# A two-block fp32 network on one core: projections merged into the differential attention, a reordered opening, and stage beginnings that run two or three tiles side by side

## The chip, the core and the metric

The kernel runs on one core of one Trainium2 chip. The metric is the device time of one execution in microseconds (us). A core has TensorE (PE in the rows: matrix products; PEld is its weight load), VectorE (DVE), ScalarE (ACT), GpSimd (POOL) and SyncE (SP, which starts DMAs). Each engine works through its own instructions in their order and waits on semaphores. TensorE's clock has two levels, 1.2 and 2.4 GHz; "granted clock" is its mean share of full speed in a stretch.

## The reference

Everything is fp32, batch 1, 256 tokens, width 1024. Cut to what matters:

```python
# block one
xn = rmsnorm(h, norm_mix_g)
q_a, k_a, v_a, q_b, f_b, i_b, og_b, g_a, g_b = split_cols(xn @ w_in)      # nine projections of 1024
y_a = moba_attention(q_a, k_a, v_a, positions) @ w_br_attn                 # "attention A": 16 heads of 64, causal, rope
y_b = hgrn2(q_b, f_b, i_b, og_b, lb, hgrn_norm_g) @ w_br_hgrn              # gated linear recurrence, 8 heads of 128
h = h + (sigmoid(g_a) * y_a + sigmoid(g_b) * y_b) @ w_out
h = h + memory_cross_attention(rmsnorm(h, g_x), rmsnorm(mem, g_mem), wq_x, wkv_x, wo_x)   # 4 heads of 256
hn = rmsnorm(h, norm_ffn_g)
h = h + (silu(hn @ w_gate) * (hn @ w_up)) @ w_ffn_out
x2 = rmsnorm(h, final_norm_g)
# block two, layer 0: differential attention over 256 tokens and 256 context tokens
q, k, v, z = split(adaln_norm(t) @ w_in0)          # for the tokens and for the context
o = softmax(q1 k1) v - lam * softmax(q2 k2) v      # 8 heads, two softmaxes of 64 each
o = rms_norm(o, subln_g) * (1 - lam_init)
y = (o * silu(z)) @ w_out0
# block two, layer 1: 8 query heads on 2 key heads (GQA), then the same gating and w_out1
```

## The kernel before

Activations lie feature-major: [128 partitions, k, tokens], with k = 0..7 the eight slices of 128 features. A projection of 1024 features is eight **tiles** (t = 0..7), each a weight piece of 128 x 1024. An fp32 product is made of three fp32r products: w_hi by X_H, w_hi by X_L, w_lo by X_H (L1040 to L1042), where H is the operand cast to fp32r and L the rest. A tile is so 8 x 3 = 24 products, 256 columns wide, or 512 where tokens and context go together (names W in block two). A weight piece lands in a ring of seven buffers (w_raw), ScalarE casts w_hi (L1263), VectorE subtracts w_lo (L1450), into a ring of four; tiles are summed in three PSUM banks named lin.

The program is one list, `steps`. Each engine walks the whole list in its order and carries out what is its own in each step. So the place of a step in the list is its place in every engine's queue. Steps are: "lin" (a tile, with its evacuation: a copy, a scaling "R", silu, gating, and so on), "gain" and "shift" (making the operand H and L of one k), "sq"/"sqmm" (squares and their sums), "rt" (GpSimd's power for the norm), "bc", "rope", "score_mm", "score_exp", "pscale", "transp", "values", "values_out", "headn", "zgate". Weights are split ahead of use: at the lin step of a tile, the tiles up to two further are split, and this split stands ahead of the tile's own evacuation; with `HL` four pieces can be live.

`bc` spreads a norm's 1/rms over all partitions: VectorE multiplies the identity by the 128 values (L1568, tile diag), TensorE multiplies ones by that (L1116), VectorE copies the result to rstd (L1570).

The opening makes eight gain steps (XH, XL), 8 x 2 sums of squares, then q_a; after its first tile a "setup" step makes the rope's angles, sines and the attention's lambda. Ropes of q_a's tiles stand in q_a, those of k_a's in k_a. An attention is a pipeline over (head, part): while one softmax is scaled and transposed, the scores of the next are made, and `fill()` puts other work between "values" and "transp". In attention A `fill_w` puts three tiles of q_b ... g_b into each head until the 44 tile steps are used up. HGRN then has 14 rounds (`htake`), each followed by one tile of k_x or v_x; the operand of mem (eight gains, MH, ML) is made before. `pending` holds evacuations put off by one round.

In block two all of q_2, k_2 and v_2 stand ahead of the differential attention, whose `fill_da` holds only norm steps; its scores use a ring of four banks. All z_2 tiles come after, each evacuated through silu and the gating with the head's output (zgate: L1527, L1491, L1492, 512 wide, making ZH and ZL), then w_out0 twice (the two halves st of 256 tokens), q_3, k_3, v_3, the GQA attention with z_3 in it, eight gates, and w_out1. TensorE waits for all eight gates of w_out0 at once, and in w_out1's first tile for one gate per k. Where a tile's operand has just been made, the first tile waits for each k in turn.

## Time and profile before

| | us |
|---|---|
| median of 3 runs | 1445.77 (1445.62 to 1447.35) |
| profiled execution, its own time | 1446.14 |
| its span in the trace | 1444.4 |
| TensorE busy | 1262.5 (87%) |
| VectorE busy | 819.7 (57%) |
| ScalarE busy | 598.8 (41%) |
| differential attention with q_2, k_2, v_2 before it and z_2 behind | 850.8 to 1179.5 |

Times in the trace count from the span's start. "Stretches" give, for a window, each engine's busy time and TensorE's granted clock; timeline rows give one instruction, or a run of like ones, with the idle time of its engine before it and the instruction that ended it.

### The profile page before, as it was taken

To read this page: it belongs to the slowest core of one execution; us is meant where nothing else is said; L and a number is where in the kernel's file an instruction comes from. 1 tells how busy PE (TensorE), PEld (TensorE's weight loads), DVE (VectorE), ACT (ScalarE), POOL (GpSimd) and SP (SyncE) were. 2 spreads that over 40 slices of the span, in tenths; PEclk is the share of its full clock that TensorE was granted. 3 is DMA by queue.
4 is the path that set the end of the run, shared out by engine and by line. 5 is a ranking of instruction groups with operands and counts; after the bars stand their busy time and mean duration, and the time that the engine had idled before them with its cause. 6 is when DMAs were issued, how large, how long until landed. Compare 5 with 4: busy or idle time off the path is not lost.

```text
span 1444.4 us, 22626 instructions
## 1 busy us (share of the span) xinstructions
PE 1262.5 (87%) x8530; PEld 1116.0 (77%) x8530; DVE 819.7 (57%) x1604; ACT 598.8 (41%) x1077; POOL 53.4 (4%) x51
## 2 busy tenths in 40 slices
PE   4999998988875998999998979998776899888886
PEld 4998997978874997988897968895333679887766
DVE  4755554659655755565665444425777445575563
ACT  4864445451311343433333335634444235454452
POOL 0000000002021000000000000000000000001000
PEclk9999999998987999999999979998887899879988
DMA  6454443442311452488865722230000124312110
GB/s 234 145 170 148 134 148 128 139 139 72 104 59 44 149 177 74 132 292 292 293 229 214 258 87 89 101 103 30 1 0 1 44 90 158 103 59 74 62 42 30
DMA packets 48395, 175.01 MB, mean 121 GB/s; under 512 B 5376, under 2 KB 6016, under 8 KB 47776
## 3 DMA queue, kind: packets, MB, share of 16 engines
q1 hardware_dynamic: 47664, 169.77, 34.7%
q0 software_dynamic: 624, 3.80, 0.7%
q8 instruction: 69, 1.13, 0.3%
q14 instruction: 38, 0.31, 0.1%
HBM read 172.50 MB, written 1.05 MB: 120 GB/s over the span
## 4 chain that ended last, share of the span: by engine, by line
PE 38%; issue 11%; DVE 7%; ACT 2%; POOL 0%; ACTq 0%; POOLq 0%; DVEq 0%
PE lin L1040 10%; PE lin L1042 9%; PE lin L1041 9%; PE sum_bank L1104 1%; DVE stat L1692 1%; PE lin L1055 1%; PE lin L1057 1%; PE lin L1056 1%; PE o_bank L1153 1%; PE score L1073 1%; PE sum_bank L1116 1%; ACT probs L1385 1%; DVE probs L1716 1%; DVE diag L1568 0%; DVE probs L1635 0%
## 5 line engine op out<-in xcount | busy, mean ns | idle before, releaser
L1450 DVE TENSOR_TENSOR w_lo<-w_raw,w_hi 128x1024 fp32r<-128x1024 f32 (+1 forms) x272 | 328.5, 1213 | 225.4 <-ACT w_hi L1263 185.6
L1263 ACT CAST w_hi<-w_raw 128x1024 fp32r<-128x1024 f32 (+1 forms) x272 | 275.5, 1036 | 120.3 <-PE lin L1042 87.2
L1040 PE MATMUL lin<-XH,w_hi 128*128 128x256 f32 x448 | 131.5, 293 | 3.2 <-DVE w_lo L1450 3.1
L1041 PE MATMUL lin<-XL,w_hi 128*128 128x256 f32 x448 | 128.8, 287 | 0.0
L1042 PE MATMUL lin<-XH,w_lo 128*128 128x256 f32 x448 | 128.7, 287 | 0.0
L1040 PE MATMUL lin<-NH,w_hi 128*128 128x256 f32 x416 | 121.5, 292 | 0.0
L1041 PE MATMUL lin<-NL,w_hi 128*128 128x256 f32 x416 | 119.0, 286 | 0.0
L1042 PE MATMUL lin<-NH,w_lo 128*128 128x256 f32 x416 | 118.9, 286 | 0.0
L1104 PEld LDWEIGHTS sum_bank<-ones,sqr 128*128 128x128 f32 x368 | 55.5, 225 | 49.5 <-ACT sqr L1297 48.9
L1040 PEld LDWEIGHTS lin<-XH,w_hi 128*128 128x128 f32 x448 | 88.2, 197 | 7.1 <-issue 6.7
L1104 PE MATMUL sum_bank<-ones,sqr 128*128 128x2 f32 x368 | 55.6, 266 | 40.6 <-ACT sqr L1297 40.2
L1040 PEld LDWEIGHTS lin<-NH,w_hi 128*128 128x128 f32 x416 | 80.9, 194 | 12.7 <-issue 12.6
L1041 PEld LDWEIGHTS lin<-XL,w_hi 128*128 128x128 f32 x448 | 88.1, 197 | 0.0
L1042 PEld LDWEIGHTS lin<-XH,w_lo 128*128 128x128 f32 x448 | 88.0, 196 | 0.0
L1042 PEld LDWEIGHTS lin<-NH,w_lo 128*128 128x128 f32 x416 | 81.1, 195 | 0.0
L1041 PEld LDWEIGHTS lin<-NL,w_hi 128*128 128x128 f32 x416 | 81.0, 195 | 0.1
L1040 PE MATMUL lin<-WH,w_hi 128*128 128x512 f32 x192 | 78.7, 410 | 2.7 <-DVE WL L1608 2.7
L1041 PE MATMUL lin<-WL,w_hi 128*128 128x512 f32 x192 | 76.5, 398 | 0.0
L1042 PE MATMUL lin<-WH,w_lo 128*128 128x512 f32 x192 | 76.4, 398 | 0.0
L1219 POOL TENSOR_TENSOR ms<-ms,mhalf 128x4 f32<-128x4 f32 (+1 forms) x26 | 26.2, 1008 | 1300.8 <-DVE ms L1558 1300.8
L1385 ACT ACTIVATE probs<-score,stat 128x512 f32<-128x512 f32 (+1 forms) x56 | 34.6, 621 | 69.2 <-DVE stat L1697 42.7
L1143 PE MATMUL pt_bank<-ident,probs 128*128 128x128 f32 x224 | 39.1, 299 | 24.0 <-DVE probs L1721 22.0
(350 smaller groups left out, 3231.4 us busy)
## 6 DMA issues: line engine op xcount, KB each, us to landing
w_raw<-in_ada SPq DMA_DIRECT2D x48, 512.0 KB, 5.6
w_raw<-in_w_out SPq DMA_DIRECT2D x32, 512.0 KB, 3.3
w_raw<-in_gate SPq DMA_DIRECT2D x22, 512.0 KB, 6.0
w_raw<-in_up SPq DMA_DIRECT2D x22, 512.0 KB, 3.9
w_raw<-in_ffn_out SPq DMA_DIRECT2D x16, 512.0 KB, 4.2
w_raw<-in_q SPq DMA_DIRECT2D x16, 512.0 KB, 4.1
w_raw<-in_z SPq DMA_DIRECT2D x16, 512.0 KB, 3.3
w_raw<-in_k SPq DMA_DIRECT2D x10, 512.0 KB, 3.2
```

The costliest lines, as they stand in the source:

```text
L1040: nc.tensor.matmul(bank[:, 0:W], wh, moving(H, kk), start=first, stop=False)
L1041: nc.tensor.matmul(bank[:, 0:W], wh, moving(L, kk), start=False, stop=False)
L1042: last = nc.tensor.matmul(bank[:, 0:W], wl, moving(H, kk), start=False, stop=final)
L1055: nc.tensor.matmul(o, xh, wh, start=(k == 0), stop=False)
L1056: nc.tensor.matmul(o, xh, wl, start=False, stop=False)
L1057: last = nc.tensor.matmul(o, xl, wh, start=False, stop=(k == DT - 1))
L1104: last = nc.tensor.matmul(bank[:, c0 + 2 * tt:c0 + 2 * tt + 2], src, ones[:, 0:2], start=(s["k"] == 0 and tt == 0), stop=(s["k"] == s["K"] ...
L1143: last = nc.tensor.transpose(pt_bank[:, d0:d0 + P], src[:, c0:c0 + P], ident[:, :])
L1219: nc.gpsimd.tensor_tensor(rt[:, n, 0:w], ms[:, n, 0:w], mhalf[:, 0:1].broadcast_to([P, w]), ALU.pow)\
L1263: scal.copy(w_hi[:, i % HL, 0:n], raw[:, tile["i"] % RAW, 0:n]).then_inc(w_hi_ready, 1)
L1385: ins = scal.activation(dst, dst if mask is not None else u["bank"][:, c0:c0 + w], ACT.Exp, bias=stat[:, 0, i % 4, j:j + 1], scale=u["scal ...
L1450: vec.tensor_sub(w_lo[:, i % HL, 0:n], raw[:, tile["i"] % RAW, 0:n], w_hi[:, i % HL, 0:n].bitcast(F32)).then_inc(w_lo_ready, 1)
```

## The change

1. `bc` loses VectorE's diag product (26 of them): TensorE multiplies the 1/rms column, broadcast to 128 x 128, by the identity, one 128-wide product for each 128 tokens, and waits for GpSimd directly.
2. Opening: the five constants are loaded by GpSimd's queue; a small copy stands first on ScalarE; the gain steps look ahead less (so w_hi and w_lo stand between them); the squares go into q_a tiles 2 to 5; angles into q_a 1 to 3 and sines behind q_a 5; lambda into v_a; the ropes of q_a's tiles go into k_a, two per tile, and the last ones into v_a.
3. Attention A holds 36 tile steps, spread evenly over its 16 heads. The eight g_b tiles go into HGRN rounds 0 to 7, then the sigmoid of g_b and the gains of mem, then k_x and v_x two per round.
4. The first two tiles of q_x, and gate 0 and up 0, are issued ahead of "bc" with their evacuations put off.
5. Differential attention: q_2(0), k_2(0), v_2(0), q_2(1) come first; all other tiles stand in the attention's 24 steps: part 0 of head h has k_2(h+1) and the ropes of Q and K, part 1 two value tiles (h < 3) or a z_2 tile, part 2 q_2(h+2) or z_2. z_2 is stored raw in K2; one tile of it remains behind. The ring of score banks is two. The gates are made in halves: half 0 of all eight tiles before w_out0, half 1 two each at w_out0's tiles 2 to 5.
6. `together` marks two or three tiles, and TensorE runs them side by side: q_a, br_hgrn, w_out0 (half 0), q_3, w_out1 with three tiles, q_2 with k_2, k_3 with two. For each k all members' products follow each other; before the first, it waits for the banks and for w_hi and w_lo of all members; the ring slots are freed at the end.

The core of the diff:

```diff
+        def together(stage, ts):
+            members = [s for kind, s in steps if kind == "lin" and (s["stage"], s["t"]) in [(stage, t) for t in ts]]
...
         def fill_da():
...
+            if part == 0 and nxt < DA_HEADS:
+                rope_2(Q2, nxt)
+                wide_2("k_2", nxt, K2)
+                rope_2(K2, nxt)
+                roped_2.append(n_rope[0])
+            elif part == 1 and nxt < DA_HEADS:
+                if h < 3:
+                    values_2(2 * h + 2)
+                else:
+                    gate_early(len(z_early))
+            elif part == 2 and nxt + 1 < DA_HEADS:
+                wide_2("q_2", nxt + 1, Q2)
+            elif len(z_early) < 7:
+                gate_early(len(z_early))
...
         for t in range(8):
-            lin_step("z_2", t, DT, True, W2, 2 * T, ("zgate", Q2, ZH, ZL))
...
+            gate_half(0, t)
...
+            if t == 2:
+                together("w_out0", range(3))
+            if 2 <= t < 6:
+                gate_half(1, 2 * t - 4)
+                gate_half(1, 2 * t - 3)
...
+            def side_by_side(members):
...
+                for s in members:
+                    if s["g"] >= NLIN:
+                        pe.wait_ge(lin_out[s["g"] % NLIN], s["g"] // NLIN)
+                    pe.wait_ge(w_hi_ready, s["pieces"][0]["s"] + 1)
+                    pe.wait_ge(w_lo_ready, s["pieces"][0]["s"] + 1)
...
+                for k in range(DT):
+                    if op["ops"] is not None:
+                        pe.wait_ge(op_ready, op["ops"][k])
+                    if "gates" in first:
+                        pe.wait_ge(gate_used, first["gates"] + k + 1)
+                    for s in members:
...
+                        last = nc.tensor.matmul(bank[:, 0:W], wl, moving(H, k), start=False, stop=k == DT - 1)
+                        if k == DT - 1:
+                            last.then_inc(w_used, 1)
```

**VectorE in the differential attention**, at the step with the norm of a head (part 0). Before, from the broadcast's diag on (Q_116 is the tile of queries and head outputs, o_bank the values' bank, probs the softmax):

```order
L1568 TENSOR_TENSOR diag<-ident,ms 128x512
L1570 COPY rstd<-sum_bank 128x512
L1653 SCALAR_TENSOR_TENSOR Q_116<-Q_116,lamt,rstd 128x512
L1738 COPY Q_116<-o_bank 128x512
L1709 RECIPROCAL stat<-stat 128x1 x2
L1713 TENSOR_SCALAR stat<-stat,lamt 128x1
L1716 TENSOR_SCALAR probs<-probs,stat 128x512
L1721 SCALAR_TENSOR_TENSOR probs<-probs,stat 128x512
L1692 TENSOR_REDUCE stat<-lin 128x1 x2
```

After, the same step (Q_115 and K_116 are the tiles of q_2 and k_2, tab_63 the rope's table):

```order
L1824 TENSOR_TENSOR Q_115<-Q_115,tab_63 128x256
L1825 TENSOR_TENSOR rot<-rot,tab_63 128x256
L1826 TENSOR_TENSOR Q_115<-Q_115,rot 128x256
L1596 TENSOR_TENSOR w_lo<-w_raw,w_hi 128x1024
L1824 TENSOR_TENSOR K_116<-K_116,tab_63 128x256
L1825 TENSOR_TENSOR rot<-rot,tab_63 128x256
L1826 TENSOR_TENSOR K_116<-K_116,rot 128x256
L1718 COPY rstd<-sum_bank 128x512
L1801 SCALAR_TENSOR_TENSOR Q_115<-Q_115,lamt,rstd 128x512
L1886 COPY Q_115<-o_bank 128x512
L1857 RECIPROCAL stat<-stat 128x1 x2
L1861 TENSOR_SCALAR stat<-stat,lamt 128x1
```

The diag product has gone; the two ropes (six passes) and a w_lo stand ahead of rstd, and so ahead of the scaling of probs.

**VectorE from the last z_2 tile to w_out0.** Before (rot holds silu of z_2, ZH and ZL are w_out0's operand; the nine w_lo are those of w_out0):

```order
L1450 TENSOR_TENSOR w_lo<-w_raw,w_hi 128x1024
L1527 TENSOR_TENSOR rot<-rot,Q_116 128x512
L1491 CAST ZH<-rot 128x512
L1492 TENSOR_TENSOR ZL<-rot,ZH 128x512
L1450 TENSOR_TENSOR w_lo<-w_raw,w_hi 128x1024 x9
L1558 TENSOR_SCALAR ms<-pt_bank 128x2
L1450 TENSOR_TENSOR w_lo<-w_raw,w_hi 128x1024
```

After, the last gate of half 0, 256 wide, and the first of half 1:

```order
L1699 TENSOR_TENSOR rot<-rot,Q_115 128x256
L1645 CAST ZH<-rot 128x256
L1646 TENSOR_TENSOR ZL<-rot,ZH 128x256
L1596 TENSOR_TENSOR w_lo<-w_raw,w_hi 128x1024 x3
L1699 TENSOR_TENSOR rot<-rot,Q_115 128x256
L1645 CAST ZH<-rot 128x256
L1646 TENSOR_TENSOR ZL<-rot,ZH 128x256
```

Eight gates stand in a row, and the next three w_lo, of which the first is that of w_out0's third tile, stand behind the eighth. On ScalarE the w_hi of tile 3 stands behind the evacuation of tile 0.

**VectorE in the opening.** Before (XL is the operand's rest, one pass for each k):

```order
L1450 TENSOR_TENSOR w_lo<-w_raw,w_hi 128x1024 x2
L1583 SCALAR_TENSOR_TENSOR XL<-xT,cols,XH 128x256 x8
L1450 TENSOR_TENSOR w_lo<-w_raw,w_hi 128x1024
L1558 TENSOR_SCALAR ms<-sum_bank 128x2
L1456 TENSOR_SCALAR lamt<-cols 128x1
L1458 CAST cs_65<-rot 128x256
```

After:

```order
L1731 SCALAR_TENSOR_TENSOR XL<-xT,cols,XH 128x256 x3
L1596 TENSOR_TENSOR w_lo<-w_raw,w_hi 128x1024
L1731 SCALAR_TENSOR_TENSOR XL<-xT,cols,XH 128x256 x3
L1596 TENSOR_TENSOR w_lo<-w_raw,w_hi 128x1024
L1731 SCALAR_TENSOR_TENSOR XL<-xT,cols,XH 128x256 x2
L1596 TENSOR_TENSOR w_lo<-w_raw,w_hi 128x1024 x2
L1604 CAST cs_64<-rot 128x256
L1605 TENSOR_SCALAR rot<-cs_64,cols 128x256
```

The weights' w_lo stand between the passes of the operand, and the angles (cs_64, rot) behind four of them.

## Rows read from the trace of the kernel before

**Rows 1.** The page: its span, TensorE's busy time, exponentials, w_hi (count, busy, mean ns, idle).
```profile
span 1444.4 us, 22626 instructions
...
PE 1262.5 (87%) x8530; PEld 1116.0 (77%) x8530; DVE 819.7 (57%) x1604; ACT 598.8 (41%) x1077; POOL 53.4 (4%) x51
...
L1263 ACT CAST w_hi<-w_raw 128x1024 fp32r<-128x1024 f32 (+1 forms) x272 | 275.5, 1036 | 120.3 <-PE lin L1042 87.2
...
L1385 ACT ACTIVATE probs<-score,stat 128x512 f32<-128x512 f32 (+1 forms) x56 | 34.6, 621 | 69.2 <-DVE stat L1697 42.7
```

**Rows 2.** Stretches: start:end, length, busy (instructions) by engine, clock, DMA share, GB/s.
```profile
864.00:900.00 36.00, 36.00 (x160) 29.83 (x159) 14.80 (x27) 22.79 (x42) 0.00 (x0) 1.00 0.28 94
...
940.00:986.00 46.00, 46.00 (x385) 45.96 (x384) 11.64 (x14) 15.74 (x24) 0.00 (x0) 1.00 0.32 104
...
986.00:1122.60 136.60, 98.29 (x360) 50.97 (x358) 97.61 (x281) 58.20 (x161) 7.05 (x7) 0.80 0.00 1
...
1122.60:1179.50 56.90, 51.35 (x204) 40.24 (x204) 26.91 (x37) 13.60 (x17) 1.42 (x1) 0.91 0.21 68
...
1182.30:1193.30 11.00, 11.00 (x80) 11.00 (x81) 3.49 (x3) 3.62 (x7) 0.00 (x0) 0.84 0.28 97
...
1249.00:1254.20 5.20, 5.20 (x25) 5.20 (x26) 2.52 (x3) 1.64 (x4) 0.70 (x1) 0.50 0.79 234
```

**Rows 3.** Timeline (start, length, engine, line, operation, [idle <-releaser]), TensorE, differential attention.
```profile
1045.52 1.13 PE L1133 MATMUL score<-K,Q 64*128 64x512 f32 x4
...
1052.87 3.08 PE L1153 MATMUL o_bank<-wideT,V 128*128 128x512 f32 x8
```

**Rows 4.** Timeline of ScalarE (first row) and VectorE: a rope pass, then one softmax step.
```profile
49.43 0.42 ACT L1374 ACTIVATE rot<-Q 32x256 f32<-32x256 f32 x1
...
1057.49 0.69 DVE L1570 COPY rstd<-sum_bank 128x512 f32<-128x512 f32 x1 [1.22 <-PE sum_bank L1116]
...
1059.61 0.21 DVE L1709 RECIPROCAL stat<-stat 128x1 f32<-128x1 f32 x2
...
1061.29 0.75 DVE L1692 TENSOR_REDUCE stat<-score 128x1 f32<-128x256 f32 x2
```

**Rows 5.** Timeline of TensorE: the last squares of one norm, and the first product of w_out0.
```profile
522.55 0.61 PE L1104 MATMUL sum_bank<-ones,sqr 128*128 128x2 f32 x4 [2.54 <-ACT sqr L1297]
...
1182.30 0.36 PE L1040 MATMUL lin<-ZH,w_hi 128*128 128x256 f32 x1 [2.81 <-issue]
```

**Rows 6.** Timeline of VectorE and TensorE at the beginning of w_out1.
```profile
1396.35 0.43 DVE L1492 TENSOR_TENSOR BL<-rot,BH 128x256 fp32r<-128x256 f32 x1
...
1396.92 0.36 PE L1040 MATMUL lin<-BH,w_hi 128*128 128x256 f32 x1 [1.73 <-DVE BL L1492]
...
1404.56 1.22 DVE L1450 TENSOR_TENSOR w_lo<-w_raw,w_hi 128x1024 fp32r<-128x1024 f32 x1
```

**Rows 7.** Timeline of VectorE at the beginning of br_hgrn.
```profile
469.08 1.22 DVE L1450 TENSOR_TENSOR w_lo<-w_raw,w_hi 128x1024 fp32r<-128x1024 f32 x1
```

**Rows 8.** Timeline of ScalarE and TensorE: the opening, and attention A's first score.
```profile
9.92 1.04 ACT L1263 CAST w_hi<-w_raw 128x1024 fp32r<-128x1024 f32 x1 [7.90 <-DMA w_raw<-in_q_a]
...
22.65 0.56 PE L1040 MATMUL lin<-XH,w_hi 128*128 128x256 f32 x1
...
109.48 1.12 PE L1133 MATMUL score<-K,Q 64*128 64x128 f32 x8 [1.13 <-ACT V L1320]
```

**Rows 9.** Stretches of attention A and of HGRN, and timeline rows in HGRN.
```profile
109.50:294.60 185.10, 174.71 (x1328) 160.50 (x1329) 100.06 (x233) 83.82 (x144) 0.00 (x0) 0.98 0.44 139
...
322.90:374.00 51.10, 43.21 (x330) 42.83 (x331) 47.60 (x72) 12.24 (x17) 11.88 (x8) 0.90 0.25 82
...
323.18 3.27 DVE L1583 SCALAR_TENSOR_TENSOR ML<-memT,cols,MH 128x256 fp32r<-128x256 f32 x8
...
340.37 1.22 PE L1116 MATMUL sum_bank<-diag,ones 128*128 128x256 f32 x2 [3.67 <-DVE diag L1568]
...
398.72 2.04 PE L1176 MATMUL pt_bank<-qk 128*128 128x128 f32 x8 [3.21 <-issue]
```

More of the change, by code:

```diff
@@ L532, in program @@
             evac_pending()
-            if kv:
-                n, t, ev, feat = kv.pop(0)
-                lin_step(n, t, DT, feat, MW, T, ev)
-                if n == "k_x" and t == 0:
-                    bc_with(NM)
+            if todo_gb:
+                n, t, ev, feat = todo_gb.pop(0)
+                lin_step(n, t, DT, feat, XW, T, ev)
+            elif len(mem_ops) < DT:
+                if not mem_ops:
+                    steps.append(("gates", {"g": n_lin[0] - 1, "sig": [gb], "silu": []}))
+                for k in range(DT):
+                    gain_step(k, memT[:, k, :], "norm_mem", MH[:, k, :], ML[:, k, :])
+                    mem_ops.append(n_op[0])
+            for _ in range(2 if len(mem_ops) == DT else 0):
+                if kv:
+                    evac_pending()
+                    n, t, ev, feat = kv.pop(0)
+                    lin_step(n, t, DT, feat, MW, T, ev)
+                    if n == "k_x" and t == 0:
+                        bc_with(NM)
             if i % ROUNDS == ROUNDS - 1:
@@ L544, in program @@
         evac_pending()
+        assert not kv
         defer[0] = False
@@ L556, in program @@
         feat8("br_hgrn", operand(HH, HLo, ops=ops), ("gate_b", None))
+        together("br_hgrn", range(3))
         def residual(stage, op, kts, gain, H, L, beside=None, ada_each=0):
@@ L570, in residual, with first_two @@
                     ops.append(n_op[0])
+            return N, operand(H, L, ops=ops) if gain else None
+        def first_two(N, first, second):
+            defer[0] = True
+            first()
             rt_step(N)
-            return N, operand(H, L, ops=ops) if gain else None
+            second()
+            bc_step(N)
+            evac_pending()
+            defer[0] = False
         N3, op3 = residual("w_out", operand(GH, GL), DT, "norm_x", NH, NL)
@@ L582, in q_x @@
             lin_step("q_x", q_todo.pop(0), DT, True, op3, T, ("R", QX, N3))
+        first_two(N3, q_x, q_x)
         q_x()
-        bc_with(N3)
-        for _ in range(3):
-            q_x()
+        q_x()
         def head_x(h):
@@ L795, in program @@
             beside(t, 1)
+        together("q_3", range(3))
         W3 = operand(W3H, W3L, True, ops3[1])
@@ L802, in program @@
             late = {"sq": lin_sq[0], "N": k_norms[t], "t": None}
+        together("k_3", range(GQ_KV))
         def k_ready(t):
@@ L855, in program @@
             lin_step("w_out1", t, DT, True, operand(BH, BL), T, ("act", YB))
+            if t == 0:
+                steps[-1][1]["gates"] = 2 * DT
             sq_step(NZ, t, YB[:, t, :], DT, ("g", n_lin[0] - 1), "late")
+        together("w_out1", range(3))
         rt_step(NZ)
@@ L1101, in sq @@
                         pe.wait_ge(rstd_ready, s["n_bc"])
+                    if s["m"] and not own:
+                        pe.wait_ge(tables_act, 2)
                 for tt in range(s["tts"]):
@@ L1322, in linear @@
                         ins.then_inc(free, 1)
-                elif ev[0] == "silu":
-                    after_lin(act, g)
-                    r = rot[:, s["slot"] % 2, 0:W]
-                    scal.activation(r, r, ACT.Silu).then_inc(silu_done, 1)
+                elif ev[0] == "silu" and not s["later"]:
+                    silu(s)
                 elif ev[0] == "zgate":
```

285 lines of the change are left out of this document (176 added, 109 removed).

## The prediction

> **What bounds the kernel now.** I read the first lines of the page, then the stretches view for the clock and the busy time of each engine in each stage, then the timeline at the places the diff touches. TensorE is busy 87% of a span of 1444.4 us [rows 1]; the profiled execution took 1446.14 us, within 0.03% of the median 1445.77, so a sum made on it holds for the median as well. The reader is to see two kinds of stretches. In a projection stage alone, 256-wide products follow each other every 46.00/385 = 0.12 us and 512-wide ones every 36.00/160 = 0.225 us, at a granted clock of 1.00, with VectorE and ScalarE half idle [rows 2]: a tile of 24 products is 2.83 or 5.4 us, and nothing but fewer products makes it shorter. In the differential attention (986 to 1122.6) TensorE is busy 98.29 of 136.60 us at clock 0.80 and VectorE 97.61 [rows 2]: small products wait for softmax steps, and after the waits the array runs at its lower level. After an idle stretch the clock is 0.50 and 25 products take 5.20 us, twice as long [rows 2]. Time can therefore be won only where TensorE idles or runs at 1.2 GHz.
>
> **Differential attention merged with its projections: −54.** Before, 135.2 us of q_2/k_2/v_2 (850.8 to 986), 136.6 of attention and 56.9 of z_2 follow each other [rows 2], 328.7 in all. TensorE's work at full clock: 24 wide tiles x 5.4 = 129.4; eight value tiles x 5.66 = 45.3; attention 8.2 per head, 65.3 for eight. That is counted at full clock: four score products of a third of a head 1.13 with the tail of the last, 0.85 without, three times; eight products for the values 3.08, 2.56 without the tail [rows 3]; twelve transposes, the norm's sums and its broadcast another 3.1. (98.29 busy at clock 0.80 would be 78.6, since tails and half-rate products are in it; that end adds 13.) Sum 240: the floor. Now what comes on top.
> The start: q_2 and k_2 of tile 0, two value tiles, q_2(1) are 10.8 + 11.3 + 5.4 = 27.5, half clock at first +2.3, copy and first split 1.4, ropes before the first score 2.9: 34.1.
> A steady head needs 3 x 5.4 + 8.2 = 24.4 on TensorE. Of its three steps the first is longer on the other two engines: from k_2's end ScalarE copies (0.6) and makes four 32-partition rope passes of 0.42 [rows 4], 1.7; VectorE then ropes (1.3) and takes rstd 0.69 [rows 4], headn and values copy about the same (0.75, 0.69), scaling 1.7 to 2.0 (from 1059.61 to 1061.29 [rows 4]), row maxima 2 x 0.75 [rows 4] and ScalarE's exponentials 2 x 0.62 [rows 1]: 10.6 against TensorE's 8.0. That stall of 2.6, and 1.2 where the other steps' transposes wait behind a w_hi and a copy on ScalarE, give 28.2. Three heads with two value tiles in place of a wide one take 31.3. Head 7 and z_2(7) take 23 + 8.4. Sum 34.1 + 3 x 31.3 + 4 x 28.2 + 31.4 = 272; head 0, whose softmax has nothing beside it yet, adds 2: 274 against 328.7. The floor (240, gain 89) and rival D below are the bounds. VectorE has 18 to 20 us of work per head and ScalarE 15.5, both under 28. The ring of four score banks becomes two; the tile step between two scores is longer than an exponential (0.62), so I cost it at nothing. Its cover is that tile; without it each step pays up to 1.2.
>
> **w_out0: +14.5.** Before, the first product stands at 1182.30, 2.8 behind z_2's end [rows 5], and three tiles take 11.00 [rows 2]: tile 3 starts at T+13.8 (T is the end of z_2). After, all eight gates of half 0 come behind z_2's end. A gate is three 128x256 passes; eight follow each other in the present w_out1, 1.12 each (seven from the end of the first to the w_lo at 1404.56) [rows 6]. First gate about T+2.5 (sum, broadcast, headn), eighth T+11.5. The order shows the w_lo of the third tile only behind them, and the group's first product waits for the weights of all three: T+12.7. Its 72 products take 10.8 (5.0 at half rate, 49 at full). Then evacuation 0.4, square 0.4, w_hi 1.04 [rows 1], w_lo 1.22 [rows 6] before tile 3, because those stand behind tile 0's evacuation in ScalarE's order: T+26.6, and another 1.5 for a clock that falls in the idle 3 us. 26.6 + 1.5 − 13.8 = 14.3, taken as 14.5. The bound below is the gates alone: −3.7, if the third w_lo did not wait.
>
> **w_out1: +8.** Same form. Tile 0 now starts at 1396.92, when one gate is done [rows 6], and works beside the gates; the w_lo at 1404.56 stands right behind the last BL [rows 6]. The group starts there, 1405.9, ends 1416.7, tile 3 at 1419.8 against 1413.3; +1.5 for the clock.
>
> **br_hgrn: +3.** The third w_lo is at 469.08 [rows 7], behind the eight gates on VectorE, with TensorE at work on tile 0 meanwhile. In the changed order the gates end about 4.4 earlier (no diag, shorter form); the group starts 464.7, ends 475.5, tile 3 at 478.5 against 477.3, plus half clock. **q_3, k_3: −1.5**: the group of q_3 starts at 1250.4, about where half of its products were done before, but the second and third tile no longer run at clock 0.50 behind a wait (5.20 us [rows 2]).
>
> **Opening: −5.** The first w_hi waits 7.90 us for its DMA [rows 8] and the first projection stands at 22.65, behind 32 small sums [rows 8]. With the sums late the group of q_a can start near 15.3, when the gains are done. It loses some: 2.7 for tile 3 (as above), and ropes of Q moved into k_a make that stage ScalarE-bound: per k_a tile two ropes 3.3, copy 0.4 and w_hi 1.04 are 4.8 against 2.83 on TensorE, seven times, 13.8, which the same ropes cost in q_a before as well (3 and 1 per tile) and k_a's then (1 per tile). I take the first score from 109.48 [rows 8] to 104.5. The five constants go to the GpSimd queue, off SyncE's issue. The Trainium skill (DMA: Bandwidth & Descriptors, Issuing engines are not separate DMA queues) says that the same 16 engines serve all of them; by it the first weight lands no earlier, and no run of before shows otherwise, nor do I count a gain there.
>
> **Attention A and HGRN: −1.** Attention A holds 44 steps in 185.10 us, TensorE busy 174.71 [rows 9]: it is full, so eight g_b tiles less make it 22.6 shorter, 162.5. They go into HGRN rounds 0 to 7, where in 322.9 to 374 TensorE has 43.21 and VectorE 47.60 of 51.10 [rows 9]: full as well, so they cost 22.6 there, less 2 hidden. The 3.27 of the gains of mem at 323.18 with TensorE idle, and the idle 3.67 before the diag [rows 9], go (−6.5); one sigmoid, eight gains without a tile beside them and a falling clock come (+7). Rounds 8 to 11 hold stalls (3.21 at 398.72 [rows 9], clock 0.90); two k_x tiles in each fill some of them. Net 21.5 against 22.6.
> **q_x −3.9, gate/up −2.6, broadcasts −2, end −0.5.** The first tile of q_x now stands around the last squares, which cost 2.54 of idle at 522.55 [rows 5] plus a broadcast wait; the same at the FFN's head. 26 diag passes of 0.5 to 0.7 leave VectorE; only in the chains of two norms does TensorE wait for one, 2 us together.
>
> **Sum**: 54 + 5 + 1 + 6.5 + 2 + 1.5 + 0.5 − 14.5 − 8 − 3 = 45. 1446.1 − 45 = **1401 us**.
>
> **Rivals.** (B) The groups do not pay for gathered waits: the third w_lo finds room between gates, since the products are the same and side by side they cannot run before the operand anyway. Then w_out0 costs 3.7, w_out1 gains 2.3, br_hgrn 5, q_3 another 8, some 37 better: 1364. For it: TensorE waits 1.73 before w_out1 with one gate done [rows 6], so it starves today. Against it: a w_lo's place in VectorE's order is fixed, and today's rows 1404.56 and 469.08 show it behind the last gate. Chance 0.18.
> (D) The merged steps stall 1 us more each: 23 steps, 1424. For it: every rope, copy and w_hi now stands in one line with the exponentials, and the waits before transposes, on VectorE's scaling, are today's own pattern. Chance 0.18.
> (Slower) The steps do not overlap at all. Each of 23 steps would have to lose 1.9 us beyond what I counted, since 44/23 = 1.9; then the stage keeps 328.7 and the groups' 25 remain beside 16 of other gains: 1455. The point is where projection tile, scaling and copy run one behind the other through two score banks. TensorE busy 72% against 5.4 us of independent products speaks against it. Chance 0.05.
> (G) The moved g_b tiles fall into idle time after all; 10 better, 1391. It lies inside the range.
> A rule on the clock bears on the groups. The rows first: behind the idle 2.81 before w_out0 the next 11.00 us have a clock of 0.84, behind the starved first tile of q_3 it is 0.50 for 5.20 us [rows 2, 5]. The Trainium skill (TensorE: Matmul & The Clock Gate, HAM oscillation — how this bites in real kernels) has bursts with waits between them restart cold each time, which speaks against collecting short waits into one long idle. With it the groups cost what I wrote; without it each group is 2.5 cheaper, three groups 7.5, 1394.
>
> **Chances.** Forecast 0.55 (with G), B 0.18, D 0.18, slower 0.05, the small remainder between. The range reaches over D and half of B's way: 1372 to 1430. A measurement of this kernel tells 0.2%, 3 us, from no change; faster by more 0.95, within it 0.01, slower 0.04.
>
> **What would show it.** First projection at about 15, attention A about 162 us long, the differential part 274 with a clock near 0.95 and TensorE over 85% busy; w_out0's first product 12 to 13 us behind the last z_2 product, with the third w_lo directly behind eight gates; a gap of 3 us before tile 3 of each group. If the differential part takes 290 or more, D holds; if the groups start early, B. Wrong would be: a stall on the value tiles that wait for a ring slot of w_hi, or a first score later than 109.

## The result, and the profile after

| | before | after |
|---|---|---|
| median, us | 1445.69 (1444.27 to 1447.35) | 1432.34 (1431.72 to 1433.17) |
| ratio, 95% interval | | 0.9908 [0.989, 0.9925] |
| span of the profiled execution | 1444.4 | 1430.2 |

The change makes the kernel 0.9% faster: 13 us, where 45 were forecast (1401 us, range 1372 to 1430). From the page of the changed kernel, its span, TensorE's busy time and the granted clock in 40 slices:

```profile
span 1430.2 us, 22790 instructions
...
PE 1239.1 (87%) x8638; PEld 1116.7 (78%) x8638; DVE 806.8 (56%) x1602; ACT 600.9 (42%) x1094; POOL 56.9 (4%) x56
...
PEclk9989999999897899999999979999999789789988
```

The stretches of the changed kernel (attention A; HGRN rounds 0 to 7; the start of the differential part, from its first product to the first score, and from there to the first transposes; one steady head; the whole part), columns as in [rows 2]:

```profile
115.90:280.60 164.70, 151.71 (x1136) 137.73 (x1137) 87.75 (x217) 75.73 (x136) 0.00 (x0) 0.97 0.41 131
...
308.10:353.00 44.90, 41.52 (x344) 40.52 (x344) 43.51 (x62) 6.27 (x6) 11.85 (x8) 1.00 0.29 94
...
849.70:884.30 34.60, 32.23 (x168) 28.11 (x168) 14.10 (x24) 13.48 (x23) 0.00 (x0) 0.87 0.19 62
...
884.30:896.20 11.90, 10.12 (x33) 6.59 (x33) 7.08 (x17) 7.67 (x15) 0.00 (x0) 0.86 0.15 44
...
1019.60:1047.50 27.90, 26.92 (x127) 19.76 (x126) 17.84 (x44) 14.87 (x34) 1.01 (x1) 1.00 0.14 47
...
849.70:1136.00 286.30, 272.66 (x1376) 213.04 (x1376) 157.28 (x371) 136.56 (x296) 8.06 (x8) 0.94 0.18 60
```

The steady head is 27.90 us with TensorE busy 26.92 at clock 1.00, where the unmerged attention had 98.29 of 136.60 at 0.80 [rows 2]. The whole part is 286.3 instead of 328.7 (285.4 to the end of the last z_2 tile, 1135.15; the rest is the last broadcast). But the stretch from 884.3 to 896.2 is 11.9 us that belong to no steady head. Rows of its beginning: the first value tile (ScalarE's copy of q_2 and w_hi, TensorE's first product), and then, within the stretch, the second group of scores:

```profile
862.81 0.59 ACT L1457 COPY Q<-lin 128x512 f32<-128x512 f32 x1 [6.35 <-PE lin L1183]
863.29 1.05 ACT L1403 CAST w_hi<-w_raw 128x1024 fp32r<-128x1024 f32 x1
...
865.80 0.55 PE L1145 MATMUL lin<-w_hi,WH 128*128 128x256 f32 x1 [2.35 <-DVE w_lo L1596]
...
887.21 1.12 PE L1265 MATMUL score<-K,Q 64*128 64x512 f32 x2 [1.78 <-ACT probs L1531]
```

The copy of q_2 waits for the end of the q_2/k_2 group, and the w_hi of the value tile stands behind that copy, so TensorE waits 2.35 us. The second row of scores waits 1.78 us until an exponential frees one of the two score banks; four later ones wait 0.98 each.

The opening, SyncE, TensorE and ScalarE: the issue of the first weights and the first w_hi, then the first product of the q_a group, the beginning of a k_a tile, three of the operations ScalarE does for that tile, the first product of v_a, the first score (before: [rows 8]):

```profile
1.65 2.36 SPq L1051 DMA_DIRECT2D w_raw<-in_q_a  x4
...
8.50 1.04 ACT L1403 CAST w_hi<-w_raw 128x1024 fp32r<-128x1024 f32 x1 [0.65 <-DMA w_raw<-in_q_a]
...
15.88 0.55 PE L1181 MATMUL lin<-XH,w_hi 128*128 128x256 f32 x1 [15.88 <-DVE w_lo L1596]
...
69.24 0.36 PE L1130 MATMUL lin<-XH,w_hi 128*128 128x256 f32 x1 [1.63 <-DVE w_lo L1596]
...
71.46 1.05 ACT L1403 CAST w_hi<-w_raw 128x1024 fp32r<-128x1024 f32 x1
...
72.42 0.36 ACT L1457 COPY K<-lin 128x256 f32<-128x256 f32 x1
...
72.81 0.42 ACT L1520 ACTIVATE rot<-K 32x256 f32<-32x256 f32 x1
...
88.17 0.55 PE L1145 MATMUL lin<-w_hi,XH 128*128 128x256 f32 x1 [6.35 <-DVE w_lo L1596]
...
115.86 1.12 PE L1265 MATMUL score<-K,Q 64*128 64x128 f32 x8 [1.13 <-ACT V L1468]
```

The first product of q_a stands 6.8 us earlier than before (15.88 against 22.65 [rows 8]), and TensorE reaches the first score 6.4 us later (115.86 against 109.48). At 69.24 it has waited 1.63 for w_lo; between two w_hi, ScalarE does a copy and eight rope passes of 0.4. The issue of the first weights before:

```profile
4.06 8.66 SPq L961 DMA_DIRECT2D w_raw<-in_q_a  x8
```

w_out0, VectorE, TensorE and ScalarE: the first of eight gates, the last ZL of the eight, the third w_lo, the group's first product, the w_hi of tile 3, tile 3:

```profile
1137.60 0.43 DVE L1699 TENSOR_TENSOR rot<-rot,Q 128x256 f32<-128x256 f32 x1
...
1146.25 0.42 DVE L1646 TENSOR_TENSOR ZL<-rot,ZH 128x256 fp32r<-128x256 f32 x1
...
1146.59 1.22 DVE L1596 TENSOR_TENSOR w_lo<-w_raw,w_hi 128x1024 fp32r<-128x1024 f32 x1
...
1148.15 0.55 PE L1181 MATMUL lin<-ZH,w_hi 128*128 128x256 f32 x1 [12.12 <-DVE w_lo L1596]
...
1158.91 1.03 ACT L1403 CAST w_hi<-w_raw 128x1024 fp32r<-128x1024 f32 x1
...
1161.40 0.36 PE L1130 MATMUL lin<-ZH,w_hi 128*128 128x256 f32 x1
```

The group starts 13.0 us behind the end of z_2 (1135.15) and 12.12 behind the last broadcast, as the third w_lo comes directly behind the eighth gate. The beginning of k_3, the last operand pass, the second member's w_lo and the group's first product:

```profile
1267.66 0.49 DVE L1756 SCALAR_TENSOR_TENSOR W3L<-probs,ada,W3H 128x256 fp32r<-128x256 f32 x1 [0.18 <-ACT W3H L1509]
...
1268.65 1.23 DVE L1596 TENSOR_TENSOR w_lo<-w_raw,w_hi 128x1024 fp32r<-128x1024 f32 x1 [0.51 <-ACT w_hi L1403]
...
1270.13 0.76 PE L1181 MATMUL lin<-W3H,w_hi 128*128 128x512 f32 x1 [7.91 <-DVE w_lo L1596]
```

And the two places where TensorE waits for w_lo in ffn_out (before 2.21 us at 774.02, on the same transfer) and in w_out1 (before 1.73 at 1396.92 [rows 6]):

```profile
771.82 0.55 PE L1130 MATMUL lin<-FH,w_hi 128*128 128x256 f32 x1 [4.76 <-DVE w_lo L1596]
...
1385.84 0.55 PE L1181 MATMUL lin<-BH,w_hi 128*128 128x256 f32 x1 [10.82 <-DVE w_lo L1596]
```

Counted as the start of the same tile in both kernels, the difference after minus before runs: first score +6.4; end of attention A −14.0; last HGRN rounds +1.0; w_out +3.6; FFN −1.0; differential part begins −1.1, its last z_2 ends −44.3; w_out0's fifth tile −30.4; q_3's last tile −31.9; v_3's last −19.9; w_out1's tile 3 −13.6; end −14.2. So the differential part won 43.2, and w_out0 13.9, k_3 12.0 and w_out1 6.3 were given back. (Two expectations below still have 43.6 and 14.3, with the end of z_2 read 0.4 us off.)

### The profile page after: what moved, and what is told of

It reads as the page before. It is cut to its first block and busy times, and to the rows that moved or that the text cites. A ratio compares the mean times of both kernels' runs of the same rounds, so it can differ in the third digit from the quotient of the medians.

```text
span 1430.2 us, 22790 instructions
## 1 busy us (share of the span) xinstructions
PE 1239.1 (87%) x8638; PEld 1116.7 (78%) x8638; DVE 806.8 (56%) x1602; ACT 600.9 (42%) x1094; POOL 56.9 (4%) x56
## 5 line engine op out<-in xcount | busy, mean ns | idle before, releaser
L1130 PE MATMUL lin<-XH,w_hi 128*128 128x256 f32 x424 | 124.4, 293 | 7.1 <-DVE w_lo L1596 7.1
L1131 PE MATMUL lin<-XL,w_hi 128*128 128x256 f32 x424 | 121.1, 286 | 0.0
L1132 PE MATMUL lin<-XH,w_lo 128*128 128x256 f32 x424 | 121.0, 285 | 0.0
L1531 ACT ACTIVATE probs<-score,stat 128x512 f32<-128x512 f32 (+1 forms) x88 | 52.9, 606 | 110.8 <-DVE stat L1845 84.0
L1130 PEld LDWEIGHTS lin<-XH,w_hi 128*128 128x128 f32 x424 | 82.4, 194 | 10.9 <-issue 10.9
L1130 PEld LDWEIGHTS lin<-NH,w_hi 128*128 128x128 f32 x416 | 79.6, 191 | 14.5 <-issue 12.6
L1131 PEld LDWEIGHTS lin<-XL,w_hi 128*128 128x128 f32 x424 | 82.6, 195 | 0.0
L1132 PEld LDWEIGHTS lin<-XH,w_lo 128*128 128x128 f32 x424 | 82.4, 194 | 0.0
L1132 PE MATMUL lin<-WH,w_lo 128*128 128x512 f32 x176 | 71.4, 406 | 0.0
L1131 PE MATMUL lin<-WL,w_hi 128*128 128x512 f32 x176 | 71.4, 406 | 0.0
L1230 PE MATMUL sum_bank<-ones,sqr 128*128 128x2 f32 x368 | 51.6, 252 | 14.0 <-ACT sqr L1445 13.6
L1840 DVE TENSOR_REDUCE stat<-score 128x1 f32<-128x512 f32 (+1 forms) x88 | 48.1, 565 | 15.8 <-PE score L1265 15.8
```

The costliest lines, as they stand in the source:

```text
L1130: nc.tensor.matmul(bank[:, 0:W], wh, moving(H, kk), start=first, stop=False)
L1131: nc.tensor.matmul(bank[:, 0:W], wh, moving(L, kk), start=False, stop=False)
L1132: last = nc.tensor.matmul(bank[:, 0:W], wl, moving(H, kk), start=False, stop=final)
L1230: last = nc.tensor.matmul(bank[:, c0 + 2 * tt:c0 + 2 * tt + 2], src, ones[:, 0:2], start=(s["k"] == 0 and tt == 0), stop=(s["k"] == s["K"] ...
L1531: ins = scal.activation(dst, dst if mask is not None else u["bank"][:, c0:c0 + w], ACT.Exp, bias=stat[:, 0, i % 4, j:j + 1], scale=u["scal ...
L1840: ins = vec.reduce_max(m, src, AX_X)
```

## Experiments

Sixteen further kernels ran. Times are medians; the ratio is to the kernel before, measured with it on the same chip.

| kernel | us | ratio [95%] |
|---|---|---|
| the change | 1432.3 | 0.9908 [0.989, 0.9925] |
| e2, groups q_a and q_2/k_2 only | 1392.3 | 0.9632 [0.9618, 0.9647] |
| e3, no k_3 group | 1420.0 | 0.9825 [0.981, 0.9839] |
| e4, all groups, early splits | 1390.6 | 0.9625 [0.9609, 0.964] |
| e5, ropes spread | 1424.9 | 0.9867 [0.9846, 0.9887] |
| e6 = e4 + e5 | 1386.4 | 0.96 [0.9581, 0.9619] |
| e7, two groups, early splits, ropes | 1391.3 | 0.9631 [0.9609, 0.9653] |
| e8, e2 unmerged | 1442.4 | 0.9978 [0.9965, 0.9991] |
| e9, e2 with g_b back | 1389.9 | 0.9618 [0.96, 0.9636] |
| e10 | 1377.3 | 0.9524 [0.9509, 0.9539] |
| e11, e10 + gates at three places | 1376.2 | 0.9523 [0.9508, 0.9539] |
| e12, e2 with diag | 1426.0 | 0.9862 [0.9849, 0.9876] |
| e1, no groups | 1373.5 | 0.9504 [0.9491, 0.9517] |
| e14, q_2/k_2 group only | 1384.9 | 0.9577 [0.9561, 0.9593] |
| e15, no groups, tuned | 1370.1 | 0.9479 [0.9466, 0.9492] |
| **e13, three late groups, tuned** | **1368.1** | **0.9467 [0.9454, 0.948]** |
| e16, before without diag | 1425.8 | 0.9857 [0.9837, 0.9878] |

### What the groups cost: e2, e3, e4, e1, e14

The change has seven groups (two expectations say eight). e2 drops five `together` lines (br_hgrn, w_out0, q_3, k_3, w_out1), e3 only that of k_3 (first line). e14 drops the five of e2 and that of q_a, and e1 besides these the line that joins q_2 and k_2 (second).

```diff
-        together("k_3", range(GQ_KV))
...
-        steps[-1][1]["members"] = steps[-2][1]["members"] = [steps[-2][1], steps[-1][1]]
```

> The changed kernel with only two of its eight side-by-side groups (q_a, and q_2 with k_2); br_hgrn, w_out0, q_3, k_3 and w_out1 run tile by tile again. Theory 1 (a group gathers the waits of all its members into one idle time, measured as 2.7 + 14.3 + 12.3 + 6.6 us lost at four places and 1.5 won at q_3): about 34 us faster than the changed kernel, 1398 us. Theory 2 (the operand's own passes set these places, and a first tile that starts early only stalls product by product): within 5 us of the changed kernel, 1428 to 1432.

> Only the k_3 group is undone. Theory 1: k_3's first tile runs beside the shift passes, which end 6 us behind its possible start, and the second w_lo is no longer in its way: 8 to 12 us faster than the changed kernel, 1420 to 1424. Theory 2 (the operand sets it): under 3 us, 1430 or more.

e2 is 40.0 us faster than the change (theory 1 had 34), e3 12.4 (8 to 12). Theory 2 (the operand sets these places) is out. In e3 the first tile of k_3 starts when its first operand pieces are there, and TensorE waits 0.49 us for the second w_lo instead of 7.91 for both:

```profile
1260.26 0.47 PE L1129 MATMUL lin<-W3H,w_hi 128*128 128x512 f32 x1
...
1268.20 0.47 PE L1129 MATMUL lin<-W3H,w_hi 128*128 128x512 f32 x1 [0.49 <-DVE w_lo L1595]
```

e2 gains 7 more than the places sum to against before (2.6 + 13.9 − 1.5 + 12.0 + 6.3 = 33.3, from br_hgrn to w_out1). The price of each group is the start of the same tile in the change and in e2: br_hgrn 7.0 us, w_out0 6.7, q_3 9.0, k_3 11.1, w_out1 7.0, 41 in all. Against before the picture is another one. q_3 looked 1.5 better, because before TensorE waited 2.76 and 2.94 us there for diag; br_hgrn looked cheap for the same reason; and half of w_out0's 13.9 us is not its group but the eight gates behind z_2's end, which e2 keeps. One of the two waits in q_3 of the kernel before:

```profile
1257.80 0.89 PE L1116 MATMUL score<-diag,ones 128*128 128x256 f32 x2 [2.76 <-DVE diag L1568]
```

e4 keeps the groups and takes away what they wait for:

```diff
-            steps.append(("hgate", {"N": N, "pr": pr}))
+            steps.append(("hgate", {"N": N, "pr": pr, "look": 4}))
```

with the same `look` at the gates ahead of w_out0 (half 0) and w_out1 and at the shifts ahead of q_3 (4) and k_3 (3), so that all members' weights are split before the operand is made.

> All eight groups stay; the look-ahead of the splits is raised at the gates of w_out0, of HGRN and of w_out1 and at the shifts ahead of q_3 and k_3, so that the w_hi and w_lo of all members stand ahead of the gates. Theory 1 (the late third w_lo is what the groups wait for): groups start with the first gate; w_out0 10, k_3 11, w_out1 11, q_3 6, br_hgrn 5 us better, 43 in all, 1389. Theory 2 (the groups wait for the last operand pass anyway, and the added w_lo ahead of the gates push these back): 0 to 10 us, 1422 to 1432. Rival on the clock: the starved products run at half rate and leave half of the gain, some 20 us, 1412.

1390.6: the change less 41.8 us, as theory 1 has it (43), and not the 20 of the clock rival. In e4 too the group of w_out0 begins at half rate: its first 24 products take 4.71 us (1127.10 to 1131.81), as in the change (4.72). The groups of w_out0, q_3 and k_3 in e4 begin so:

```profile
1127.10 0.55 PE L1186 MATMUL lin<-ZH,w_hi 128*128 128x256 f32 x1 [5.18 <-DVE ZL L1651]
...
1195.87 0.55 PE L1186 MATMUL lin<-W3H,w_hi 128*128 128x256 f32 x1 [8.91 <-DVE W3L L1761]
...
1238.47 0.47 PE L1186 MATMUL lin<-W3H,w_hi 128*128 128x512 f32 x1 [0.64 <-DVE W3L L1761]
```

w_out0 waits for its first ZL alone, 5.18 instead of 12.12, k_3 0.64 instead of 7.91. q_3's still waits 8.91 (9.52 in the change), now for W3L; the added splits stand ahead of the shifts there, and that they push these back is read from the order. That is the one place where an early split only moved the wait; the runs did not separate it further.

> The changed kernel with no group at all. Against e2 this takes the groups of q_a and of q_2 with k_2 away. Theory: their members' weights are split before the operand is ready, so they fill its waits: 3 to 6 us slower than e2, 1395 to 1398. Rival (no group is worth anything): within 1 us of e2 or faster.

The expectation (3 to 6 us slower than e2) was the wrong way round: without the last two groups the kernel is 18.8 us faster, not slower. The rows of e1 (first product, first score):

```profile
11.63 0.55 PE L1122 MATMUL lin<-XH,w_hi 128*128 128x256 f32 x1 [11.63 <-DVE w_lo L1588]
...
108.17 1.12 PE L1257 MATMUL score<-K,Q 64*128 64x128 f32 x8 [1.13 <-ACT V L1460]
```

and of e2:

```profile
15.68 0.55 PE L1175 MATMUL lin<-XH,w_hi 128*128 128x256 f32 x1 [15.68 <-DVE w_lo L1590]
...
115.45 1.12 PE L1259 MATMUL score<-K,Q 64*128 64x128 f32 x8 [1.22 <-ACT V L1462]
```

q_a's group waits for the third w_lo, until 15.68, where tile 0 alone starts at 11.63 beside the gains; the first score is 7.3 us later.

> e1 plus the group of q_2 with k_2 alone, so e2 without the group of q_a. If the two groups' costs stand apart: q_a 7 to 11, q_2/k_2 4 to 8 us, so 1378 to 1381. If all 19 us are q_a's (the later differences only follow its clock): 1374.

1384.9, above both forecasts: by the medians q_a costs 7.5 and q_2/k_2 11.3. The latter is not all the group's. From 345 to 480 us, long before it, e14 and e1 run the same program (the windows count a few instructions more or less, as e14 is behind); e1 first, then e14:

```profile
345.00:480.00 135.00, 111.31 (x826) 109.10 (x827) 88.37 (x143) 37.94 (x50) 15.22 (x13) 0.90 0.33 106
```

```profile
345.00:480.00 135.00, 112.86 (x812) 110.62 (x811) 85.80 (x141) 37.95 (x50) 15.23 (x13) 0.86 0.30 100
```

The clock is 0.90 and 0.86, and by 490 us e14 is 5.7 us behind. In the differential part itself e14 takes 286.2 and e1 279.1 us: 2.35 are the wait for w_lo of the first value tile (852.45), which is absent in e1; the rest are tiles at half rate, 6.97 instead of 5.35 us. So at most 7 us belong to the group. From its first product to the first of the last z_2 tile the part takes 277.6 to 278.0 us in the change, e2, e14 and e6, 275.0 and 274.1 in e10 and e4, all with the group, and 270.4, 270.7 and 272.2 in e1, e15 and e13, without it: 2 to 8 us, of which 2.35 are the wait. For the clock elsewhere no cause was found. The traced execution of e14 is its slowest of four (1386.4) and that of e1 its fastest of five (1372.0), so part of the difference is that between executions.

### The opening: e5, and the rests of it in e6, e7

```diff
-            if 2 <= t < 6:
-                for k in (2 * t - 4, 2 * t - 3):
+            if t in (2, 3):
+                for k in range(4 * t - 8, 4 * t - 4):
...
-            rope_some(2 if t else 0)
+            rope_some(1)
             lin_step("k_a", t, DT, True, XW, T, ("act", K))
```

with rt and bc two tiles earlier, one rope in q_a's tiles 6 and 7, and two per step in v_a.

> The opening only: the squares stand two tiles earlier, and the ropes are spread, one per tile from q_a's tile 6 on over k_a, two per step in v_a. Theory 1 (k_a is bound by ScalarE: two ropes, copy and w_hi are 4.7 us per tile, one rope makes 3.1): seven tiles x 1.6 and most of the 6.4 us gap ahead of v_a, 12 to 15 us faster than the changed kernel, 1417 to 1420. Rival (the weights' DMA sets k_a's pace): within 3 us, 1430.

7.4 us, against 12 to 15: the first value tile starts at 79.39 instead of 88.17, but inside v_a TensorE now waits 1.8 us twice for w_lo, and the first score is 6.2 us earlier (109.67). The k_a stage was bound by ScalarE; two ropes per step look too many in v_a as well. This price holds beside q_a's group: e15, which spreads the ropes without any group and has g_b back, is only 3.5 us faster than e1.

> All eight groups, the early splits of e4 and the spread ropes of e5 together. If the two gains (41.7 and 7.4 us against the changed kernel) are independent: 1383 us. Rival (time won in the opening is given back at the next transfer or weight wait): 1388 or more.

> As e6 but with the two groups q_a and q_2/k_2 alone. Theory (side by side is worth little once the splits stand early; its gain of a group over tiles one by one is what a starved first tile leaves idle, 1 to 3 us at each of five places, paid back by the falling clock): 1381 to 1387. Rival (a group fills the operand's waits with three tiles instead of one, 3 to 5 us at each place): e7 is 10 to 20 us slower than e6.

e6 gains 4 us over e4, not 7, between its two forecasts. e7 is 5 us slower than e6, where its theory had it level and its rival 10 to 20 slower, and no better than e2. By the starts of the same tiles it is 4.9 us ahead of e2 at the first score, by the ropes, and 3.9 behind it at the end: early splits without groups lose some 9 us by these traces (e7's is its slowest execution and e2's its fastest) and 4 by the medians, most of it in q_3. That the w_lo ahead of the gates and shifts delay the first of them was not tested by itself. Early split and group belong together.

### The merging and the diag product: e8, e12, e16

> The kernel of e2 (two groups) with the differential attention unmerged: all of q_2, k_2 and v_2 ahead, all z_2 behind, raw; ring of two score banks and gates in halves as in the changed kernel. By the trace of before the parts are 135.2 + 136.6, and z_2 without the gates between its tiles 45 instead of 56.9: 317 against the 285 of the merged form, so 32 us slower than e2, 1424. If the whole 43.6 us belong to the merging, 1436. If the ring of two costs where nothing stands between the scores (24 steps, up to 1.2 each), up to 1453.

e8 puts q_2, k_2 and v_2 ahead and z_2 behind again in e2's code. It is 50 us slower, where 32 were expected, and inside the bound for the ring. Its attention and z_2:

```profile
981.00:1128.00 147.00, 114.75 (x398) 65.42 (x396) 95.24 (x275) 59.37 (x162) 7.05 (x7) 0.72 0.00 1
...
1128.00:1175.70 47.70, 47.40 (x210) 39.03 (x210) 12.85 (x13) 10.78 (x15) 1.01 (x1) 0.96 0.27 88
```

147.0 us instead of 136.6 [rows 2] in the attention, for the ring of two banks where nothing stands between the scores: TensorE's waits for exponentials (1.78, 0.94, 0.81 us in its first steps) sum to 10.2 us, and before, with four banks, there is one of 1.52. And 47.7 instead of 56.9 in z_2. By the starts of the same tiles e8 is 1.9 us behind e2 where the part begins, 48.0 where w_out0 begins and 49.6 at the end, so the merging is worth 46 us against this form with two banks; against before, with four, the part won 43.2.

e12 restores `bc` in e2:

```diff
-                pe.wait_ge(rt_ready, s["N"]["rti"] + 1)
+                pe.wait_ge(diag_ready, s["r"] + 1)
...
+                vec.tensor_tensor(diag[:, 0:w, :], i_, r, ALU.mult).then_inc(diag_ready, 1)
```

> The kernel of e2 with the diag product back on VectorE in all 26 broadcasts. The prediction put 2 us on the chains of two norms and more on HGRN: 2 to 5 us slower than e2, 1394 to 1397. Rival (hidden everywhere): within 1 us.

33.7 us slower, where 2 to 5 were expected. In the merged attention diag stands in VectorE's order behind the ropes of K, these behind ScalarE's passes, and these behind the tile's evacuation; TensorE waits at the broadcast. ScalarE's last rope pass, VectorE's last one and diag, then TensorE, in e12:

```profile
1025.12 0.40 ACT L1513 COPY rot<-K 32x256 f32<-32x256 f32 x1
...
1026.34 0.42 DVE L1825 TENSOR_TENSOR K<-K,rot 128x256 f32<-128x256 f32 x1
...
1026.68 0.68 DVE L1715 TENSOR_TENSOR diag<-ident,ms 128x512 f32<-128x512 f32 x1
...
1027.42 2.07 PE L1235 MATMUL sum_bank<-diag,ones 128*128 128x512 f32 x2 [4.36 <-DVE diag L1715]
```

and the same broadcast in the changed kernel, which follows the tile without a wait:

```profile
1018.73 1.05 PE L1241 MATMUL sum_bank<-ident,ms 128*128 128x128 f32 x8
```

There are five such waits of 4.3 us. By the starts of the same tiles the differential part brings 20 us, q_3's norms 9, and all that stands before block two 5.

> The kernel of before with the new broadcast alone (no diag product on VectorE). The prediction's terms for it: 2 us in the chains of two norms, some 4 us of idle before the diag in HGRN, 0 in the differential attention: 5 to 8 us faster than before, 1438 to 1441. Theory from e12 (34 us lost with the diag in the merged kernel, 22 of them at five places of 4.3 us in the merged attention): in the unmerged kernel the diag stands behind no rope and no w_lo, so those 22 are not to be had here: 1434 to 1440. Rival (the diag costs as much here): 1412.

e16 is the kernel before with the new `bc` alone:

```diff
+                    last = nc.tensor.matmul(s["N"]["bank"][:, tt * P:(tt + 1) * P],
+                                            rt[:, s["n"], tt:tt + 1].broadcast_to([P, P]), ident[:, :],
...
-                vec.tensor_tensor(diag[:, 0:w, :], i_, r, ALU.mult).then_inc(diag_ready, 1)
```

It takes 1425.8 us, 19.4 us faster and faster than the whole change. The traced execution (1422.6) ends 24 us ahead of that of before. By the starts of the same tiles HGRN's first broadcast gives 4.4 of it, the end of HGRN 3.3, the two broadcasts ahead of br_hgrn 5.5 (they stood at waits of 3.58 and 4.08 us), the differential part with z_2 3, and q_3 8 to 10; 2 are lost again ahead of block two. The expectation (5 to 8, or up to 11) was short, and the rival (33) was too high. So on top of the new broadcast all the other parts of the change together cost 6.5 us; without the groups, in e1, they win 52.

### Attention A and HGRN, and the best version: e9, e10, e11, e13, e15

e9 puts the tiles of g_b back into attention A:

```diff
-        todo_gb = [("g_b", t, ("R", gb, NX), True) for t in range(8)]
+        todo_gb = []
```

with g_b in A's list and one tile of g_a or k_x instead of two per later HGRN round.

> The kernel of e2 with the eight g_b tiles back in attention A and one k_x or v_x tile per HGRN round. The traces of before and after give attention A 20.4 us for the tiles taken out and HGRN 16 us for them: about 4 us slower than e2, 1396. Rival (the move gave nothing): within 1 us.

e9 was expected 4 us slower than e2 and is 2.4 us faster, with intervals that overlap: moving g_b into HGRN wins nothing. VectorE and TensorE are both near full in rounds 0 to 7, before [rows 9] and after.

e10 joins the edits that had gained: e5's ropes, e9, and the groups of br_hgrn, w_out0 and w_out1 with early splits:

```diff
-            steps.append(("hgate", {"N": N, "pr": pr}))
+            steps.append(("hgate", {"N": N, "pr": pr, "look": 4}))
+        together("br_hgrn", range(3))
```

e11 also cuts the gates' sigmoid and silus into three steps.

```diff
-                if n == "og_b" and t == 7:
+                if t == 7 and n in ("q_b", "f_b", "og_b"):
```

> What the runs so far favour, together: groups at q_a, q_2/k_2, br_hgrn, w_out0 and w_out1, the last three with the early splits; q_3 and k_3 tile by tile with the splits where the changed kernel has them; ropes spread as in e5; g_b back in attention A as in e9. Against e2 (1392.3): br_hgrn, w_out0 and w_out1 some 2 to 3 us each, ropes 3 to 7, g_b 2: 1377 to 1383. Rival (these small gains are swallowed by the next weight wait or by a clock that falls elsewhere): 1386, as e6.

> As e10, and the silu and sigmoid of q_b, f_b and og_b, which stand in one block of 8.1 us on ScalarE in attention A and leave TensorE idle for 8.4 us (7.0 in e9), stand at three places, each behind its own eight tiles. Theory (each block is 4.5 us with its table loads and mostly covered by the tiles in flight): 4 to 6 us faster than e10. Rival (each block stops the attention's exponentials and TensorE waits 2 to 3 us at each): no change.

e10 is 15 us faster than e2, at the fast end of its forecast; e11's gates at three places, expected 4 to 6 us faster, change nothing measurable (0.9523 against 0.9524), as its rival had it.

e13 is e10 without the groups of q_a and q_2/k_2; e15 is e11 without any:

```diff
-        together("q_a", range(3))
...
-        steps[-1][1]["members"] = steps[-2][1]["members"] = [steps[-2][1], steps[-1][1]]
```

> e10 without the groups of q_a and of q_2 with k_2; the groups of br_hgrn, w_out0 and w_out1 stay, with their early splits. If q_a's group costs what the traces of e1 and e2 show (first score 108.2 against 115.5, 7.3 us; q_2 with k_2 another 3 to 7): 1377 - 10 to 14 = 1363 to 1367. Rival (q_a's loss was the late squares, which the spread ropes already mend): 1372 or more.

> No group at all, ropes spread, g_b back in attention A, the silu and sigmoid of attention A at three places. Against e1 (1373.5): ropes 3 to 7, g_b 2, gates 1 us: 1363 to 1368. Against e13 it tells what early-split groups are worth once q_a and q_2/k_2 are out: 2 to 3 us at each of three places if e4 and e10 read right, so 5 to 9 us slower than e13; rival: the same.

e13 is the fastest kernel, 1368.1 us, 5.3% faster than before and 64 us faster than the change; e15, without any group, is 1.9 us slower with intervals that overlap. Both missed their forecasts on the slow side (e13 by 1 us, e15 by 2), and the 5 to 9 us between them did not come: by the two intervals the three early-split groups lie between 1 us lost and 4 us won.

## Why the prediction was wrong

The direction was right and most mechanisms too; the sum was 31 us too good. Three terms carry it: k_3, put at nothing (12.0), the opening (11.4) and the differential attention (10.8); the others come to 3 the other way. In the first two a group waits for all its members' inputs, at k_3 at a place that was overlooked, in the opening priced against the wrong start; a group has its part in the third as well. Point by point:

- **k_3, 0: measured +12.0.** "q_3, k_3: −1.5" looked only at q_3. The mechanism was the one named for w_out0; its fourth place was overlooked, since before TensorE does not wait there at all (e3: 12.4 us). And q_3's −1.5, measured −1.5, is luck: the reason given was the clock of its second and third tile, but its group costs 9.0 us (e2), and the two waits for diag that went (2.76 and 2.94 us, with what followed) paid for it.
- **Opening, −5: measured +6.4.** Two steps failed, and the first score at 115.86 is the sign of being wrong that the prediction named ("later than 109"). "Which the same ropes cost in q_a before as well" is false: with one rope per tile ScalarE needs 3.1 us against 2.83, with two 4.7; only the second form binds (e5: 7.4 us). And the earlier start of the group was priced against the old start behind 32 sums, not against tile 0 alone, which starts at 11.63 (e14 against e2: 7.5 us); without the group the first score comes at 108.17, 1.3 us earlier than before. The term counted at nothing was not nothing: with the constants off SyncE's queue the issues of q_a begin at 1.65 and not at 4.06, behind five issues of 0.42 to 0.48, and the first w_hi stands at 8.50 instead of 9.92 [rows 8]. The Trainium skill (DMA: Bandwidth & Descriptors, Issuing engines are not separate DMA queues) says that another issuing engine saves the sequencer's time alone. By that the trace agrees, and the prediction's reading of it ("lands no earlier") was wrong by 1.4 us. The group, which starts only at 15.88, hides it.
- **Differential attention, −54: measured −43.2.** The numbers of the parts hold: the start to the first score 34.6 (forecast 34.1), heads with value tiles 30.1 to 31.9 (31.3), the others 27.9 and 29.5 (28.2), the tail 31.2 (31.4). One term failed outright, "adds 2" for head 0: between its first score and its first transposes lie 11.9 us at clock 0.86, a pipeline step with a wait of 1.78 and a tile at half rate. The sum counted 24 steps as seven heads and a tail, and left the filling of the pipeline out. But two matches are luck. The start holds a wait of 2.35 and tiles at half rate that the q_2/k_2 group brings and that the prediction put at nothing; without the group it is 30.5 in e1, and the filling 10.3. A stall on the value tiles was its other sign of being wrong. And the steady head was summed as 24.4 of work and 3.8 of stalls behind ropes and scaling; measured are 26.9 of TensorE busy and one wait of 0.98, which comes from the ring of two score banks, "costed at nothing".
- **w_out0 +14.5, w_out1 +8, br_hgrn +3: measured +13.9, +6.3, +2.6.** By steps: first product T+13.0 (forecast 12.7), tile 3 T+26.3 (26.6), a gap of 2.6 before it (3). The places of w_hi, w_lo and gates in the order decided it, as forecast against rival B. The kernel of rival B can be had, though: e4 gives it by splitting early.
- **Attention A and HGRN, −1: measured −5.4, of which e9 leaves nothing to the move.** A fell by 20.4 (forecast 22.6), HGRN rose by 15.0; but with g_b back the kernel is no slower. The other part of the gain is the diag product: in e16 it alone gives 4.6 us up to the same point.
- **q_x, gate/up, −6.5: measured −4.6; broadcasts, −2: measured 0.** In ffn_out the bc wait of 1.98 us went, and the next w_lo arrived no earlier: TensorE waits 4.76 at 771.82, before 2.21 at 774.02. The wait was handed on. Elsewhere the price of diag was badly low: e12 and e16 give 34 and 19 us.

On the clock: behind the idle 12.12 us the first 24 products of w_out0's group take 4.72 us and the second 24 2.87; tile 3, behind a gap of 2.6, begins at full rate, falls to half after 1 us and takes 4.44, and the window from 1136.0 to 1161.4 has a clock of 0.73. The Trainium skill (TensorE: Matmul & The Clock Gate, HAM oscillation — how this bites in real kernels) has bursts with waits between them restart cold; for the group behind the long wait the trace agrees. But e4, whose group starts just as slowly and gains 41.8 us, shows that the gathered wait itself, not the clock behind it, is what the groups cost.

## What to carry to other kernels

A group that first waits for all its members' inputs turns several small waits into one long one. The three late groups whose inputs were ready in time cost nothing measurable here, and won 4 us at most; so move the preparation ahead of the operand's passes together with the group, or leave the tiles one by one. Price a change against the same kernel with that part left out, not against the kernel before: here five groups looked 33 us dear beside the kernel before and were 40. And a small product that another engine waits for costs what stands ahead of it in its engine's order, not its own 0.7 us: removing it alone was worth more than the whole change.
